# Two edits to VectorE's program order at the joints between head pairs

## The chip, the core and the metric

The kernel runs on one core of a Trainium2 chip. The metric is the device time in microseconds (us) of one execution. Each engine (TensorE for matmuls, VectorE, ScalarE, GpSimd, and SyncE, which issues the DMAs) runs its own list of instructions strictly in the order in which the program writes them; the engines meet only through semaphores, so an instruction that waits holds back everything behind it on its engine.

## The reference

One decoder block over 1024 tokens of 1024 channels, in float32. The input is normalised and projected once; the columns of that projection feed three kinds of attention heads of 64 channels and a gate.

```python
h = rms_norm(x, g_in); proj = h @ w_in
qA, kA, vA, qB, kB, vB, qM, gate, qI, kI, wI = split(proj)
oA = dilated_mixture_attention(qA, kA, vA, slopes_a)   # 8 heads, causal, three (window, dilation) patterns
oB = dsa_attention(qB, kB, vB, qI, kI, wI, slopes_b)   # 4 heads, causal, top 256 keys of an indexer; shared k, v
oM = memory_attention(qM, kM, vM)                      # 4 heads over 256 memory tokens
o = concat(oA, oB, oM) * silu(gate)
out = rms_norm(x + o @ w_out, g_final)
```

Each attention is a softmax over scores plus a distance penalty, times the values.

## The kernel before

**Steps.** After an opening part (norms, transposes, indexer scores; until about 130 us) the 16 heads are worked off in eight pairs, p = 0 to 7, in the order M0, A0, A1, A2, A3, B0, B1, M1. Each pair has eight steps, i = 0 to 7, one for each tile of 128 queries: step s = 8p + i. A causal pair has i + 1 tiles of 128 keys in position i, a memory pair always two. A step with over four key tiles is called wide; its probabilities are transposed in two chunks. All engines loop over the steps, and each has its own hand-written order in a step.

**TensorE** in step s (L1663 to L1697): the scores of s (`scores`, L1528; it waits until VectorE has taken in both halves' scores of s - 1), then the transposes of the probabilities of s - 1 (`turn_prob`, chunk 0), then projection work that belongs to a later pair (`fill`, L1403, 24 matmuls; where s - 1 has two chunks, 12 matmuls, `turn_prob` of chunk 1, 12 matmuls), then the values of s - 1 (`values`, L1567; needs the transposed probabilities copied to SBUF), and after each fourth step the transposes of the inverse sums (`turn_sums`).

**Which projection falls in which step** (`SLOT`, `projection_of_step`): the next pair's keys in positions 0 and 1, this pair's gate in 2 and 3, the next pair's values in 4 and 5, the next pair's queries in 6 and 7. Each is done in two halves of 512 tokens, b = 0 and 1, one for each step. In pair 4 the next queries lie in positions 5 and 7; pair 5 has no projection in positions 0 and 1; in pair 6 other halves lie there; pair 7 has none, its steps carry the output projection.

**The bank of a half** (`bank_ids`, L513): it accumulates in the second half of `s_ps[0]` if the step is even and has up to four key tiles, and in `j_ps` otherwise. Before `fill` writes a bank, it waits that the last half in that bank has been taken out: `wait_evacuated` waits for ScalarE's copy (semaphore `j_free`) and for VectorE's `split_low` of all halves up to that one (semaphore `j_split`). Query and key halves are kept as a high part, which ScalarE rounds, and a low part, which VectorE's `split_low` (L1108) forms as bank minus high part; for a B pair's queries it is two instructions of 64 partitions, otherwise one of 128.

**ScalarE** in step s: copies the transposed probabilities of the pair's first head (`copy_probT`, L970), takes the exponents of s for both heads (`exponent`), and takes out the projection half (`evacuate`).

**VectorE** in step s (L1327 to L1364): the masked biases of s for both heads (`add_bias`; it reads the scores and writes the negated maximum), the copy of the second head's transposed probabilities of s - 1 (`copy_probT`, L1273), in a wide step between the two biases; then the inverse sums (`invert_sums`), the first portion of the top-k choice (`choose_portions`), chunk 1's copy, `finish_group` (L1292: two products of 128 x 512, the first on TensorE's transposed sums; it releases `linv_used`, on which `turn_prob` of the next step waits), `split_low` of the step's half, and the second portion of the choice. The choice is a chain of small instructions, each waiting for the one before it; it runs from step 1 into pair 4.

**GpSimd** forms the low part of each weight tile (L711) and masks (L762, L765).

Of the kernel before, what the change touches and what calls it, by code (L numbers as in the profile page):

```python
# [19 lines left out]
NT = T // P  # L20
# [24 lines left out]
STEPS = NP * NT  # L45
# [6 lines left out]
def w_tiles():  # L52


    def q_tile(p):
        g, j, _ = PAIRS[p]
        return "q", p, [({"A": C_QA, "B": C_QB, "M": C_QM}[g] + P * j, P)]

    out = [("kIwI", None, [(C_KI, DH), (C_WI, H_I)])]
    out += [("qI", j, [(C_QI + P * j, P)]) for j in range(H_I // 2)]  # L60
    out += [q_tile(0)]
    for p, (g, j, f) in enumerate(PAIRS):
        follows = PAIRS[p + 1][:2] if p + 1 < NP else None
        if follows and follows[0] == "A":
            out += [("k", p + 1, [(C_KA + P * follows[1], P)])]
        if follows == ("B", 0):
            out += [("kvB", p + 1, [(C_KB, DH), (C_VB, DH)])]

        out += [("gate", q, [(C_GATE + P * PAIRS[q][2], P)]) for q in GATES_WITH.get(p, [p])]
        if follows and follows[0] == "A":  # L70
            out += [("v", p + 1, [(C_VA + P * follows[1], P)])]
        if follows:
            out += [q_tile(p + 1)]
    return out


W_TILES = w_tiles()
# [14 lines left out]
def query_scale(p, a):  # L92

    return -(DH ** -0.5) / (slope_of(p, a) if PAIRS[p][0] == "B" else 1.0)
# [13 lines left out]
def pair_of_step(s):  # L108
    return s // NT, s % NT


def key_tiles(s):
    p, i = pair_of_step(s)
    return MT if PAIRS[p][0] == "M" else i + 1


def chunks(s):

    n = key_tiles(s)
    return [range(c, min(c + 4, n)) for c in range(0, n, 4)]  # L120
# [18 lines left out]
def projection_of_step(s):  # L139

    p, i = pair_of_step(s)
    if p == NP - 2:
        kind, b = ENDING.get(i, (None, None))
        return (W_OF[kind], b) if kind else None
    if p == LAST_A and i in LAST_A_QUERIES:
        return W_OF["q", p + 1], LAST_A_QUERIES.index(i)
    for what, at in SLOT.items():
        if (what, p) == ("q", LAST_A):
            continue
        w = W_OF.get((what, p if what == "gate" else p + 1))  # L150
        if w is not None and w >= PRE_W and i in (at, at + 1) and (what, p) != ("gate", NP - 1):
            return w, i - at

    if (p, i) in LAST_GATE_AT:
        return W_OF["gate", NP - 1], LAST_GATE_AT.index((p, i))
    return None
# [150 lines left out]
def build_program(nc, x, mem, g_in, g_mem, w_in, w_mem, w_out, g_final, dist_tab, a_tab, out):  # L307
    with ExitStack() as ctx:
# [194 lines left out]
        use_number = {u: m for m, u in enumerate(uses)}  # L503
# [3 lines left out]
        for m, (kind, _, _) in enumerate(uses):  # L507
            if m < n_pre:
                bank_ids.append(2 if kind == "wturn" else sum(b < 2 for b in bank_ids) % 2)
            else:  # L510

                s = steps_of_uses[m - n_pre]
                bank_ids.append(3 if key_tiles(s) <= 4 and s % 2 == 0 else 0)  # L513

        def bank_of(m):
            return [j_ps[:, :], o_ps[:, :], turn_banks[4], s_ps[0][:, HALF:T]][bank_ids[m]]

        def first_token(m):


            kind, w, b = uses[m]
            return FIRST_TOPK * P if kind == "w" and W_TILES[w][0] == "qI" and b == 0 else 0
# [4 lines left out]
        def is_split(m):  # L527
            kind, w, _ = uses[m]
            if kind == "w":
                return W_TILES[w][0] in ("kIwI", "qI", "k", "kvB", "q")  # L530
            return kind == "mem" and w < 2
# [511 lines left out]
        def _(dve):  # L1043
# [64 lines left out]
            def split_low(m):  # L1108

                kind, w, b = uses[m]  # L1110
                bank = bank_of(m)
                if kind == "mem":
                    dve.wait_ge(j_free, m + 1)
                    dve.scalar_tensor_tensor(out=km[:, w, 1, :], in0=bank[:, 0:N_MEM], scalar=1.0,
                                             in1=km[:, w, 0, :].bitcast(F32), op0=ALU.mult,
                                             op1=ALU.subtract).then_inc(j_split, 1)
                    return
                what, p, _ = W_TILES[w]
                at = first_token(m)
                cut = slice(HALF * b + at, HALF * b + HALF)  # L1120
                dve.wait_ge(j_free, m + 1)

                def part(dst, rows, hi, scale=1.0):
                    return dve.scalar_tensor_tensor(out=dst, in0=bank[rows, at:], scalar=scale, in1=hi.bitcast(F32),  # L1124
                                                    op0=ALU.mult, op1=ALU.subtract)

                lower, upper, both = slice(0, DH), slice(DH, P), slice(0, P)
                if what in ("kIwI", "kvB"):
                    part(kk_b[lower, 1, cut], lower, kk_b[lower, 0, cut])
                    last = part(kk_b[upper, 1, cut], lower, kk_b[lower, 0, cut])  # L1130
                elif what == "k":
                    slot = K_SLOT[p % 2]
                    last = part(qk[both, slot + 1, cut], both, qk[both, slot, cut])
                elif what == "qI":
                    part(q_i[upper, 2 * p, cut], lower, q_i[lower, 2 * p, cut], DH ** -0.5)
                    last = part(q_i[lower, 2 * p + 1, cut], upper, q_i[upper, 2 * p + 1, cut], DH ** -0.5)
                elif PAIRS[p][0] != "B":
                    hi, lo = qk[:, Q_SLOT[p], cut], qk[:, Q_SLOT[p] + 1, cut]
                    last = part(lo, both, hi, query_scale(p, 0))
                else:  # L1140
                    hi, lo = qk[:, Q_SLOT[p], cut], qk[:, Q_SLOT[p] + 1, cut]
                    part(lo[lower, :], lower, hi[lower, :], query_scale(p, 0))
                    last = part(lo[upper, :], upper, hi[upper, :], query_scale(p, 1))
                last.then_inc(j_split, 1)
# [15 lines left out]
            for what, u, k in idx_schedule(uses):  # L1160
# [4 lines left out]
                i, h = IDX_UNITS[u]  # L1165
# [76 lines left out]
            def choose_portions(s, place):  # L1242
                for n, slot in CHOICE_AT.get((s, place), []):
                    choose(IDX_TILES[n], slot)
# [28 lines left out]
            def copy_probT(s, c):  # L1273
                g = CHUNK0[s] + c
                dve.wait_ge(pt_done[1], g + 1)
                if g >= 2:
                    dve.wait_ge(pv_done, g - 1)
                n = len(chunks(s)[c])
                dve.tensor_copy(probT[:, g % 2, 1, 0:n, :], pt_ps[1][:, 0:n, :]).then_inc(pt_ready[1], 1)  # L1279
# [43 lines left out]
            def final_norm(t):  # L1323
                dve.scalar_tensor_tensor(out=y_rows[t], in0=y_rows[t], scalar=stat[:, 3, t:t + 1], in1=gf_row,
                                         op0=ALU.mult, op1=ALU.mult).then_inc(y_final, 1)

            for s in range(STEPS + 1):  # L1327
                p, i = pair_of_step(s)
                early = FILL_OUT.get(s, (None, None, None))
                wide = s < STEPS and key_tiles(s) > 4  # L1330
                if s < STEPS:
                    add_bias(s, 0)
                if s < STEPS and not wide:
                    add_bias(s, 1)
                if s >= 1:
                    copy_probT(s - 1, 0)
                if wide:
                    add_bias(s, 1)
                if s >= 1 and (s - 1) % 4 == 3:
                    invert_sums(pair_of_step(s - 1)[0], (s - 1) % NT // 4)  # L1340
                choose_portions(s, 0)
                if early[0]:
                    add_out(*early[0])
                if s >= 1 and len(chunks(s - 1)) == 2:
                    copy_probT(s - 1, 1)
                if early[1]:
                    add_out(*early[1])
                if s == STEPS:
                    start_norm(0, 0, len(EARLY_ROWS))
                if s >= 1 and (s - 1) % 4 == 3:  # L1350
                    finish_group(pair_of_step(s - 1)[0], (s - 1) % NT // 4)
                if s == STEPS:
                    dve.wait_ge(gf_in, 16)
                    for t in EARLY_ROWS:
                        final_norm(t)
                if early[2]:
                    add_out(*early[2])
                if s < STEPS and projection_of_step(s) and is_split(use_number["w", *projection_of_step(s)]):
                    split_low(use_number["w", *projection_of_step(s)])
                choose_portions(s, 1)  # L1360
                if s in REACH_AT:
                    largest(IDX_TILES[REACH_AT[s]])
                if s in SETTLED_AT:
                    settle(IDX_TILES[SETTLED_AT[s]])  # L1364
# [378 lines left out]
```

## Time and profile before

| | us |
|---|---|
| median of 3 runs | 725.63 (723.6 to 726.18) |
| the profiled execution, its own time | 725.79 |
| its span, first to last instruction | 724.0 |
| TensorE busy in the span | 679.1 (94%) |
| VectorE busy | 422.6 (58%) |
| ScalarE busy | 333.0 (46%) |
| GpSimd busy | 146.6 (20%) |

The mean granted clock of TensorE is 0.988 of full speed. A row of the timeline gives start, duration, engine, line, output and inputs, count, and in brackets how long the engine had been idle before it and what released it.

### The profile page before, as it was taken

How to read it: one execution, taken by the hardware profiler on the slowest of the kernel's cores; microseconds unless marked ns; L12 is line 12 of the kernel's file. 1: busy time of each engine (PE TensorE's matmuls, PEld its weight loads, DVE VectorE, ACT ScalarE, POOL GpSimd, SP SyncE). 2: the span in 40 equal slices, each digit the busy share in tenths (PEclk: the TensorE clock that was granted, in tenths of full speed). 3: DMA queues.
4: the chain of work that ended last, by engine and by line, in shares of the span. 5: the costliest groups of instructions: out<-in, count | busy, mean ns of one | idle time of the engine just before them, and what ended most of it. 6: DMA issues, size and time to landing. Idle time of an engine off the chain costs nothing.

```text
span 724.0 us, 11587 instructions
## 1 busy us (share of the span) xinstructions
PE 679.1 (94%) x4287; PEld 542.6 (75%) x4287; DVE 422.6 (58%) x985; ACT 333.0 (46%) x629; POOL 146.6 (20%) x96
## 2 busy tenths in 40 slices
PE   5999999999999999999988999999999999999992
PEld 4778887777777777777766787777888777777771
DVE  3947874397788477976698564552343354122245
ACT  5777653343335443534253434653563585112224
POOL 2021110111323022221124113310111156212102
PEclk9999999999999999999999999999999999999997
DMA  8511121111311131112111121101110416510004
GB/s 297 146 47 52 30 64 24 30 29 45 88 45 44 31 88 44 30 45 88 44 31 44 32 78 49 49 2 44 44 30 20 171 52 223 166 34 23 1 34 198
DMA packets 51863, 47.71 MB, mean 66 GB/s; under 512 B 5712, under 2 KB 44640, under 8 KB 51808
## 3 DMA queue, kind: packets, MB, share of 16 engines
q1 hardware_dynamic: 51808, 46.97, 21.3%
q8 instruction: 35, 0.57, 0.3%
q14 instruction: 20, 0.16, 0.1%
HBM read 39.62 MB, written 7.34 MB: 65 GB/s over the span
## 4 chain that ended last, share of the span: by engine, by line
PE 47%; DVE 12%; issue 3%; ACT 1%; DVEq 0%; ACTq 0%
PE j_ps L1438 13%; PE o_ps L1590 6%; PE pt_ps L1564 6%; PE s_ps L1640 5%; PE s_ps L1438 5%; PE s_ps L1493 4%; PE j_ps L1640 4%; DVE unread L1193 3%; PE s_ps L1646 1%; DVE probT L1279 1%; DVE tk L1194 1%; PE j_ps L1646 1%; DVE prob L1270 1%; PE pt_ps L1612 1%; DVE tk L1196 1%
## 5 line engine op out<-in xcount | busy, mean ns | idle before, releaser
L1438 PE MATMUL j_ps<-h_hi,w_hl 128*128 128x512 f32 (+2 forms) x656 | 213.6, 391 | 3.1 <-DVE h_lo L1068 1.2
L1438 PEld LDWEIGHTS j_ps<-h_hi,w_hl 128*128 128x128 f32 (+1 forms) x656 | 121.5, 186 | 28.7 <-issue 3.1
L711 POOL TENSOR_TENSOR w_hl<-w_raw,w_hl 128x1024 fp32r<-128x1024 f32 (+1 forms) x29 | 69.1, 2384 | 330.0 <-ACT w_hl L814 311.2
L988 ACT ACTIVATE prob<-prob,nmax 128x256 f32<-128x256 f32 (+7 forms) x128 | 90.0, 704 | 85.6 <-DVE nmax L1270 70.3
L1438 PE MATMUL j_ps<-h_lo,w_hl 128*128 128x512 f32 (+2 forms) x328 | 125.5, 383 | 0.0
L976 ACT ACTIVATE probT<-pt_ps 128x512 f32<-128x512 f32 (+3 forms) x88 | 41.3, 469 | 121.5 <-PE pt_ps L1564 120.9
L1564 PE MATMUL pt_ps<-ident,prob 128*128 128x128 f32 x496 | 74.7, 283 | 10.3 <-DVE gate L1297 4.9
L1564 PEld LDWEIGHTS pt_ps<-ident,prob 128*128 128x128 f32 x496 | 55.5, 142 | 28.0 <-issue 20.9
L1438 PE MATMUL s_ps<-h_hi,w_hl 128*128 128x512 f32 x224 | 74.5, 401 | 0.9 <-ACT qk L850 0.9
L1438 PEld LDWEIGHTS j_ps<-h_lo,w_hl 128*128 128x128 f32 (+1 forms) x328 | 61.2, 187 | 11.1
L1193 DVE TENSOR_SCALAR_CACHE_REDUCE unread<-idx,tk 128x384 uint8<-128x384 f32 (+5 forms) x72 | 67.8, 942 | 1.3
L1270 DVE CUSTOM_DVE_ANT_0 prob<-s_ps,bias 128x128 f32<-128x128 f32 (+7 forms) x64 | 47.0, 753 | 24.7 <-PE s_ps L1493 20.9
L1279 DVE COPY probT<-pt_ps 128x512 f32<-128x512 f32 (+3 forms) x88 | 46.7, 530 | 15.5 <-PE pt_ps L1564 15.0
L1124 DVE SCALAR_TENSOR_TENSOR qk<-j_ps,qk 128x512 fp32r<-128x512 f32 (+2 forms) x29 | 18.4, 635 | 54.3 <-ACT qk L850 39.3
L1438 PEld LDWEIGHTS s_ps<-h_hi,w_hl 128*128 128x128 f32 x224 | 42.7, 191 | 9.6 <-ACT qk L850 1.1
L1173 DVE SCALAR_TENSOR_TENSOR idx<-prob,w_i,idx 128x384 f32<-128x384 f32 (+5 forms) x42 | 41.9, 1039 | 10.2 <-ACT prob L926 10.1
L1438 PE MATMUL s_ps<-h_lo,w_hl 128*128 128x512 f32 x112 | 44.1, 394 | 0.0
L1590 PE MATMUL o_ps<-probT,v_sb 128*64 128x128 f32 x576 | 38.6, 278 | 3.5 <-DVE probT L1279 3.5
L1590 PEld LDWEIGHTS o_ps<-probT,v_sb 128*64 128x64 f32 x576 | 30.9, 136 | 14.3 <-issue 14.1
L1270 DVE CUSTOM_DVE_ANT_0 prob<-s_ps,idx 128x384 f32<-128x384 f32 (+5 forms) x24 | 21.0, 886 | 31.9 <-PE s_ps L1493 31.9
L1493 PE MATMUL s_ps<-qk 64*128 64x512 f32 (+3 forms) x288 | 35.2, 366 | 0.0
L1640 PE MATMUL s_ps<-h_hi,w_hl 128*128 128x512 f32 x96 | 31.9, 400 | 0.0
(242 smaller groups left out, 1071.6 us busy)
## 6 DMA issues: line engine op xcount, KB each, us to landing
w_raw<-in_w_in_dram SPq DMA_DIRECT2D x27, 512.0 KB, 4.1
idx<-in_x_dram SPq DMA_DIRECT2D x8, 512.0 KB, 6.2
bias<-in_a_tab_dram SPq DMA_DIRECT2D x8, 512.0 KB, 4.5
mixed_scratch<-gate SPq DMA_DIRECT2D x12, 256.0 KB, 2.6
bias<-in_x_dram SPq DMA_DIRECT2D x4, 512.0 KB, 6.5
probT<-in_w_mem_kv_dram SPq DMA_DIRECT2D x4, 512.0 KB, 6.3
bias<-in_w_out_dram SPq DMA_DIRECT2D x4, 512.0 KB, 3.8
out_dram<-idx SPq DMA_DIRECT2D x4, 512.0 KB, 4.2
```

The source lines that it names most:

```text
L711: pool.tensor_tensor(w_hl[:, w % 2, 1, :, 0:n], raw_of(w)[:, :, 0:n], w_hl[:, w % 2, 0, :, 0:n].bitcast(F32), ALU.subtract).then_inc(w_lo_ ...
L976: act.activation(probT[:, g % 2, 0, 0:n, :], pt_ps[0][:, 0:n, :], ACT.Copy).then_inc(pt_ready[0], 1)
L988: act.activation(prob[:, a, s % 2, 0:n], prob[:, a, s % 2, 0:n], ACT.Exp, scale=-1.0, bias=nmax[:, a, s % 2:s % 2 + 1], accum_out=lsum[:, ...
L1173: dve.scalar_tensor_tensor(out=x_slice(i), in0=relu[u % 4][:, 0:n], scalar=wt, in1=x_slice(i), op0=ALU.mult, op1=ALU.add).then_inc(idx_add ...
L1193: link(dve.tensor_scalar(unread[:, 0:n], xs, level, None, ALU.is_ge, ALU.add, accum_out=count))
L1270: dve.tensor_tensor_reduce(dst, s_ps[a][:, 0:n], table, scale, 3e38, ALU.add, ALU.min, low_out).then_inc(biased[a], 1)
L1279: dve.tensor_copy(probT[:, g % 2, 1, 0:n, :], pt_ps[1][:, 0:n, :]).then_inc(pt_ready[1], 1)
L1438: last = pe.matmul(bank[0:n, at:], a[:, k, 0:n], c[:, k, HALF * b + at:HALF * b + HALF], start=(k == 0 and q == 0), stop=(k == KD - 1 and ...
L1493: last[a] = pe.matmul(banks[a][:, keys], q[rows, tile], k[rows, keys], start=(m == 0), stop=(m == 2))
L1564: last = pe.transpose(pt_ps[a][:, n, :], prob[:, a, s % 2, P * k:P * k + P], ident[:, :])
L1590: last = pe.matmul(o_ps[DH * a:DH * a + DH, at], v, probT[:, g % 2, a, n, :], start=(k == 0), stop=(k == nk - 1))
L1640: pe.matmul(bank, a[:, p, :], wo_half(c, p, b), start=(p == 0 and q == 0), stop=False)
```

## The change

In steps whose position is 0 or 1 (all such steps but s = 0, so 15 of them; none is wide) VectorE's copy of the second head's transposed probabilities of s - 1, chunk 0, stands ahead of both biases of s. And where position 7 holds the second half (b = 1) of the next pair's queries, VectorE's `split_low` of it is issued in the step after, in position 0 of the next pair, behind `finish_group`, and ahead of that step's own `split_low` if there is one. This is so at the end of pairs 0 to 5. No other engine's program changes, and no instruction is added or removed.

```diff
+            def splits_late(s):
+                p, i = pair_of_step(s)
+                piece = projection_of_step(s)
+                return i == NT - 1 and piece is not None and W_TILES[piece[0]][0] == "q" and piece[1] == 1
+
             for s in range(STEPS + 1):
                 ...
+                copy_first = s >= 1 and s < STEPS and not wide and pair_of_step(s)[1] < 2
+                if copy_first:
+                    copy_probT(s - 1, 0)
                 if s < STEPS:
                     add_bias(s, 0)
                 if s < STEPS and not wide:
                     add_bias(s, 1)
-                if s >= 1:
+                if s >= 1 and not copy_first:
                     copy_probT(s - 1, 0)
                 ...
-                if s < STEPS and projection_of_step(s) and is_split(use_number["w", *projection_of_step(s)]):
+                if s >= 1 and splits_late(s - 1):
+                    split_low(use_number["w", *projection_of_step(s - 1)])
+                if s < STEPS and projection_of_step(s) and not splits_late(s) and \
+                        is_split(use_number["w", *projection_of_step(s)]):
                     split_low(use_number["w", *projection_of_step(s)])
```

## Rows read from the trace of the kernel before

**Rows 1.** The page, part 1: engine, busy us (share of the span), instructions.

```profile
PE 679.1 (94%) x4287; PEld 542.6 (75%) x4287; DVE 422.6 (58%) x985; ACT 333.0 (46%) x629; POOL 146.6 (20%) x96
```

**Rows 2.** The waits: who waited for whom, us in total, times, longest.

```profile
DVE qk L1124 <- ACT qk L850: 42.5, 11, 6.5
PE o_ps L1590 <- DVE probT L1279: 7.5, 9, 1.8
```

**Rows 3.** The timeline around step 9, TensorE and VectorE.

```profile
200.32 0.47 PE L1438 MATMUL j_ps<-h_hi,w_hl 128*128 128x512 f32 x1
...
200.53 0.68 DVE L1124 SCALAR_TENSOR_TENSOR qk<-s_ps,qk 128x512 fp32r<-128x512 f32 x1
...
206.76 0.69 DVE L1124 SCALAR_TENSOR_TENSOR qk<-j_ps,qk 128x512 fp32r<-128x512 f32 x1 [1.51 <-ACT qk L846]
```

**Rows 4.** The timeline between steps 16 and 17, VectorE and TensorE.

```profile
274.15 0.69 DVE L1297 TENSOR_TENSOR gate<-pt_ps,gate 128x512 f32<-128x512 f32 x1 [4.54 <-PE pt_ps L1612]
...
274.99 0.42 PE L1564 MATMUL pt_ps<-ident,prob 128*128 128x128 f32 x2 [0.40 <-DVE gate L1297]
275.24 0.47 PE L1438 MATMUL j_ps<-h_hi,w_hl 128*128 128x512 f32 x1
...
275.49 0.68 DVE L1124 SCALAR_TENSOR_TENSOR qk<-s_ps,qk 128x512 fp32r<-128x512 f32 x1
```

**Rows 5.** The timeline between steps 32 and 33.

```profile
431.57 0.47 PE L1438 MATMUL j_ps<-h_hi,w_hl 128*128 128x512 f32 x1
...
431.82 1.37 DVE L1124 SCALAR_TENSOR_TENSOR kk_b<-s_ps,kk_b 64x512 fp32r<-64x512 f32 x2
```

**Rows 6.** The timeline: TensorE's stalls in steps 19, 21 and 27.

```profile
296.56 0.88 PE L1590 MATMUL o_ps<-probT,v_sb 128*64 128x128 f32 x12 [0.69 <-DVE probT L1279]
...
309.50 0.30 PE L1564 MATMUL pt_ps<-ident,prob 128*128 128x128 f32 x1 [1.52 <-DVE gate L1297]
...
374.18 0.55 PE L1590 MATMUL o_ps<-probT,v_sb 128*64 128x128 f32 x6 [1.76 <-DVE probT L1279]
```

**Rows 7.** Stretches: length, busy us of PE, PEld, DVE, ACT, POOL, granted clock.

```profile
274.20:296.50 22.30, 21.27 (x114) 16.29 (x112) 20.37 (x53) 6.72 (x17) 6.66 (x4) 1.00 0.23 60
350.40:374.10 23.70, 21.32 (x114) 16.30 (x112) 22.79 (x54) 6.70 (x17) 3.57 (x2) 1.00 0.21 57
```

**Rows 8.** The timeline between steps 48 and 49.

```profile
558.15 0.69 DVE L1301 TENSOR_TENSOR gate<-o_ps,gate 128x512 f32<-128x512 f32 x1
...
558.51 0.47 PE L1438 MATMUL j_ps<-h_hi,w_hl 128*128 128x512 f32 x1
```

**Rows 9.** The timeline of steps 40 and 41, without a projection.

```profile
482.39 1.39 DVE L1124 SCALAR_TENSOR_TENSOR qk<-j_ps,qk 64x512 fp32r<-64x512 f32 x2 [1.85 <-ACT qk L854]
...
484.24 0.69 DVE L1279 COPY probT<-pt_ps 128x512 f32<-128x512 f32 x1
...
485.07 0.63 PE L1564 MATMUL pt_ps<-ident,prob 128*128 128x128 f32 x4 [1.02 <-ACT prob L988]
...
489.09 0.69 DVE L1301 TENSOR_TENSOR gate<-o_ps,gate 128x512 f32<-128x512 f32 x1
...
490.38 0.28 DVE L1279 COPY probT<-pt_ps 128x128 f32<-128x128 f32 x1
...
490.77 0.44 PE L1590 MATMUL o_ps<-probT,v_b 128*64 128x128 f32 x4 [1.06 <-DVE probT L1279]
491.14 0.61 PE L1493 MATMUL s_ps<-kk_b,qk 64*128 64x384 f32 x4
```

**Rows 10.** The timeline of step 56, VectorE and TensorE.

```profile
602.54 1.19 DVE L1289 COPY linv<-lsum 128x512 f32<-128x512 f32 x1
603.65 0.68 DVE L1279 COPY probT<-pt_ps 128x512 f32<-128x512 f32 x1
...
604.47 0.33 PE L1590 MATMUL o_ps<-probT,v_b 128*64 128x128 f32 x2 [0.26 <-DVE probT L1279]
```

**Rows 11.** The timeline at 306 us, GpSimd and VectorE.

```profile
306.24 2.37 POOL L711 TENSOR_TENSOR w_hl<-w_raw,w_hl 128x1024 fp32r<-128x1024 f32 x1 [11.07 <-ACT w_hl L814]
...
306.26 2.37 DVE L1221 SCALAR_TENSOR_TENSOR cut<-cut 128x8 f32<-128x8 f32 x1
```

**Rows 12.** Two stretches with TensorE's clock below full, columns as in Rows 7.

```profile
375.70:379.10 3.40, 3.40 (x20) 3.03 (x17) 3.22 (x7) 3.06 (x4) 0.40 (x1) 0.50 0.02 5
...
491.70:495.10 3.40, 3.40 (x14) 2.71 (x11) 1.47 (x5) 1.57 (x5) 0.00 (x0) 0.51 0.55 148
```

## The prediction, made before the changed kernel ran

> **What bounds the kernel now.** The page's first part comes first: TensorE is busy 679.1 of 724.0 us, VectorE 422.6 [rows 1]. TensorE's program sets the time, and an edit to VectorE counts only where TensorE waits for it. So I read the waits next. VectorE waits for ScalarE's copies ahead of its query splits for 42.5 us in all [rows 2]; nobody pays for that. TensorE waits for VectorE's probability copies nine times, 7.5 us in the group with the longest [rows 2]. Then I read the timeline at each joint between two pairs, TensorE beside VectorE, to see which of these waits lie in positions 0 and 1, where the change acts. Most don't: they stand in steps 19, 21 and 27 [rows 6], which the change does not touch.
>
> **The late split.** The moved instruction releases a bank. Step 7 of a pair is odd, so the second query half accumulates in `j_ps`; position 0 is even with few keys, so its half goes to the other bank; position 1 is odd again and takes `j_ps`. The fill of position 1 therefore waits for `j_split` of the query half. Before, that split was done a step earlier. Now it stands behind `finish_group`, which itself waits for the transposed sums, the last thing that TensorE does in position 0. Between there and the fill TensorE has only a score group and a short transpose.
>
> The price is read at each joint. Between steps 16 and 17 the fill starts at 275.24. VectorE issues its next split at 275.49, right behind `finish_group` [rows 4]. That slot now goes to the query split: 275.49 + 0.68 = 276.17. From the end of a VectorE instruction to the start of the matmul that it releases the same rows give 274.99 - (274.15 + 0.69) = 0.15. The fill starts at 276.32 instead of 275.24: 1.08 late. The same at step 9: 200.53 + 0.68 + 0.15 - 200.32 = 1.04 [rows 3]; at step 33: 431.82 + 0.69 + 0.15 - 431.57 = 1.09 [rows 5], taking one instruction of 0.69 since pair 4 is an A pair; step 25 has the same gap of a quarter of a microsecond between fill and slot, so 1.08. At step 49 the queries are a B pair's, two instructions of 1.39 together [rows 9]: the slot begins 0.60 behind the start of the second product, 558.75, and 558.75 + 1.39 + 0.15 - 558.51 = 1.78 [rows 8]. In all five: 6.07.
>
> Not all of it reaches the end, since TensorE stalls later for VectorE anyway. VectorE is resynchronised at each joint (4.54 idle ahead of `finish_group` [rows 4]) and its own delay behind it is one split, 0.69, not 1.08. In steps 17 to 19 and 25 to 27 it then has no slack: 20.37 busy in 22.30 us, and 22.79 in 23.70, the rest being the gaps between chained small instructions [rows 7]. There the next stall (0.69 and 1.76 [rows 6]) shrinks by 1.08 - 0.69 = 0.39. Behind step 9 there is a pause of 1.51 for ScalarE [rows 3], so nothing comes back; I take the same for step 33. So 1.04 + 0.69 + 0.69 + 1.09 + 1.78 = 5.29. VectorE's freed 0.69 in position 7 is worth nothing: it lands in the 4.54 idle. Bounds: 4 if every joint gives back as much as steps 17 and 25 and more, 6.1 if none does.
>
> **The copy first, and steps 40 and 41.** In 12 of the 15 steps a fill of 24 matmuls or other projection work lies between the transposes and the values, and neither the copy's nor the biases' place matters: the next reader of the biases comes behind that fill. If that cover were gone, each such step would lose two biases, 0.3 to 0.8. Steps 40, 41 and 56 have no fill. In step 40 TensorE waits 1.02 ahead of its last transposes; the row names ScalarE, but VectorE's copy ends only at 484.24 + 0.69 = 484.93 and the transposes start 0.14 later, because two splits stand ahead of it from 482.39 to 483.78 [rows 9]. With the splits gone and the copy in front it starts with the transposes' end, about 483.16, and the transposes at 483.99: 1.08 earlier. The chunk 1 copy, behind biases and sums, becomes the next late one and takes back 0.42; gain 0.66. In step 41 the two splits (1.39) stand behind `finish_group` and ahead of the copy; the copy leaves the two biases (0.68) behind it. The copy comes 0.69 - 0.66 = 0.03 off where it was, so the values start as before; the biases end 0.86 later than before, and the next scores, which need them and started at 491.14, start about 0.3 late. Steps 40 and 41 together: 0.3 lost; bounds -1.1 (only the gain) and +1.4 (only the splits).
>
> Step 56: the biases end before the transposes do today, so copying first pushes both biases (0.76) behind the copy. The inverse-sum copy that follows took 1.19 against 0.43 as elsewhere, held up on its own account [rows 10]; if that hold has a fixed end, all is absorbed. Between 0 and 0.75 at the stall of 0.26 [rows 10] I take 0.2.
>
> **Sum.** 5.29 + 0.3 + 0.2 = 5.8 on the profiled execution's 725.79: 731.6. That execution is 0.16 above the median of the runs shown, so I forecast 731.5.
>
> **Rivals.**
> First, the clock. It fell to half in two stretches of 3.4 us, each behind a thin stretch of TensorE: one behind the stall of 1.76, one behind steps 40 and 41 [rows 6, 9, 12]. A fall costs half of 3.4, 1.7, where TensorE is the bound. The new stall of 1.04 to 1.78 lies 0.4 behind an existing one, so steps 9 and 49 could each draw a fall: 731.5 + 3.4 = 734.9. Against it: the stall of 1.52 in step 21 drew none [rows 6].
>
> Second, fewer collisions between VectorE and GpSimd. At 306.26 a tiny VectorE instruction lasts 2.37 and ends with GpSimd's, which had started 0.02 ahead [rows 11]; the stall of 1.52 follows from it. A shift of 0.69 in VectorE could step out of such collisions: the stalls 0.69, 1.52 and 1.76 [rows 6] would go, 731.5 - 4.0 = 727.5. It decides if GpSimd's work moves with TensorE and not with VectorE. Against it: GpSimd is released by ScalarE, which waits for VectorE's biases, so both move together.
> The Trainium skill (SBUF — State Buffer, "Who interferes with whom") says that a VectorE instruction with two SBUF inputs is fully blocked by a GpSimd instruction that reads SBUF and started first. The trace agrees by the 2.37 above. By that rule alone a shift of 0.03 us in issue order would decide over 1.5 us.
>
> Third, and on the other side: VectorE's backlog is the bound and the edits relieve it. Its place is the run of stalls in steps 11 to 29: with 0.69 less ahead of each joint the choice would run ahead and TensorE's 7.5 us of waits for copies [rows 2] would go: 731.5 - 7.5 = 724.0, not slower. It decides if VectorE has no pause ahead of `finish_group`. It has 4.54 [rows 4].
>
> Fourth, the change doesn't do what it says: the fills of position 1 are in a bank that the late split doesn't hold. Then only steps 40, 41 and 56 are left: 725.63 + 0.5 = 726.1. The bank rule read in the code speaks against it.
>
> **Chances.** Forecast 0.62, with falls of the clock 0.20, fewer collisions 0.10, backlog 0.04, no hold 0.04. 0.5%, or 3.6 us, is about what this kernel's measurement can tell from no change. Slower by more than that (above 729.3): the forecast 0.62, the clock 0.20 and 0.06 of the collisions, 0.88. Within: the other 0.04 of the collisions, the unheld case 0.04 and half of the backlog 0.02, 0.10. Faster: the other half, 0.02. The range, 727.8 to 735.2, holds the forecast with the bounds of its terms, part of the collisions and two falls of the clock; it leaves out the backlog, the unheld case and the whole gain of the collisions.
>
> **What would show it.** The timeline of the changed kernel shows in steps 9, 17, 25, 33 and 49 a first matmul into `j_ps` idle for 1.0 to 1.8 and released by VectorE's L1124 line (with a shifted number); steps 19 and 27 have smaller stalls than before; in step 40 the stall of 1.02 is gone or nearly; step 41 keeps its 1.06 or grows, and the stall ahead of the scores behind it is new. It would be wrong if the first matmuls of these steps start without a stall, or if the time between two joints changes by more than the stalls at them.

## The result and the profile after

The changed kernel is slower: 733.73 us median of 6 runs (732.8 to 734.55) against 725.9 of 6 runs of the kernel before. The ratio is 1.0099 with a 95% interval of 1.0079 to 1.0120, so 7.2 us (5.7 to 8.7) are lost. (The ratios in this document are estimated from all the runs of both kernels and are not quotients of two medians; the medians here lie 7.8 apart.) The forecast was 731.5 within 727.8 to 735.2, a loss of 5.8.

The profiled execution took 734.27 us, 8.48 more than that of before. The busy times hardly moved, so the loss is waiting and slower clock (the page: engine, busy us, share, instructions; compare [rows 1]):

```profile
PE 680.9 (93%) x4287; PEld 542.8 (74%) x4287; DVE 421.6 (58%) x985; ACT 333.3 (46%) x629; POOL 146.5 (20%) x96
```

The waits have one row that the trace before does not have, and the wait for copies is hardly changed, 8.7 against 7.5 [rows 2] (changed kernel; TensorE's and VectorE's lines below L1340 now stand 13 further down, so L1438 is L1451):

```profile
PE o_ps L1603 <- DVE probT L1279: 8.7, 8, 1.9
...
PE j_ps L1451 <- DVE qk L1124: 4.9, 5, 1.6
```

Five times, up to 1.6 us: the five joints. The timeline of the changed kernel shows them at steps 9, 17, 33 and 49; step 25 reads like step 17 (start, duration, engine, line; in brackets the idle time and its releaser). VectorE at step 9 comes first, where two L1124 stand where one stood in [rows 3]:

```profile
200.03 0.69 DVE L1301 TENSOR_TENSOR gate<-o_ps,gate 128x512 f32<-128x512 f32 x1
200.64 0.68 DVE L1124 SCALAR_TENSOR_TENSOR qk<-j_ps,qk 128x512 fp32r<-128x512 f32 x1
201.23 0.68 DVE L1124 SCALAR_TENSOR_TENSOR qk<-s_ps,qk 128x512 fp32r<-128x512 f32 x1
```

```profile
200.14 0.45 PE L1577 MATMUL pt_ps<-ident,prob 128*128 128x128 f32 x2 [0.42 <-DVE gate L1297]
201.42 0.47 PE L1451 MATMUL j_ps<-h_hi,w_hl 128*128 128x512 f32 x1 [0.82 <-DVE qk L1124]
...
277.58 0.47 PE L1451 MATMUL j_ps<-h_hi,w_hl 128*128 128x512 f32 x1 [0.85 <-DVE qk L1124]
...
298.45 0.33 PE L1603 MATMUL o_ps<-probT,v_sb 128*64 128x128 f32 x2 [0.24 <-DVE probT L1279]
...
376.68 0.33 PE L1603 MATMUL o_ps<-probT,v_sb 128*64 128x128 f32 x2 [1.70 <-DVE probT L1279]
...
435.11 0.47 PE L1451 MATMUL j_ps<-h_hi,w_hl 128*128 128x512 f32 x1 [0.85 <-DVE qk L1124]
...
565.35 0.47 PE L1451 MATMUL j_ps<-h_hi,w_hl 128*128 128x512 f32 x1 [1.55 <-DVE qk L1124]
```

The stall at 298.45 is the one that was 0.69 at 296.56 [rows 6]: here part of the hold comes back. The one at 376.68, in step 27, is nearly as long as its 1.76 of before. The next fence is TensorE in steps 40 to 42 of the changed kernel, for [rows 9]. The 1.02 ahead of the second transposes is gone (they are inside the x8), the wait ahead of the values has grown from 1.06 to 1.87, and the wait ahead of the scores is new:

```profile
486.99 1.21 PE L1577 MATMUL pt_ps<-ident,prob 128*128 128x128 f32 x8 [0.30 <-issue]
488.13 2.13 PE L1603 MATMUL o_ps<-probT,v_sb 128*64 128x128 f32 x32
...
494.08 0.48 PE L1603 MATMUL o_ps<-probT,v_b 128*64 128x128 f32 x4 [1.87 <-DVE probT L1279]
494.94 1.01 PE L1506 MATMUL s_ps<-kk_b,qk 64*128 64x384 f32 x4 [0.38 <-DVE nmax L1270]
```

And the clock (stretches of the changed kernel: length, busy us of PE, PEld, DVE, ACT, POOL, granted clock). Behind step 41 the low level of 1.2 GHz lasts twice as long as in [rows 12], and there is a new fall behind step 49; the one at 375.7 is gone:

```profile
494.40:501.10 6.70, 6.32 (x23) 4.87 (x21) 1.86 (x9) 2.67 (x9) 0.00 (x0) 0.50 0.28 73
566.10:569.40 3.30, 3.30 (x9) 2.56 (x8) 0.28 (x2) 1.06 (x4) 0.00 (x0) 0.50 0.92 344
375.70:379.10 3.40, 2.42 (x28) 2.08 (x29) 3.19 (x10) 3.37 (x7) 0.40 (x1) 1.00 0.02 5
```

How much later each stretch of steps begins than in the trace before, read from the first score matmul of the step in both traces:

| from step to step | lateness before, after it | gained or lost | what it is |
|---|---|---|---|
| start to 9 | 0, 0.11 | 0.11 | |
| 9 to 10 | 0.11, 1.11 | 1.00 | hold |
| 10 to 17 | 1.11, 1.31 | 0.20 | stall of step 11, 1.00 against 0.78 (differs from run to run) |
| 17 to 25 | 1.31, 1.92 | 0.61 | hold 1.03, given back 0.45 at step 19 |
| 25 to 33 | 1.92, 2.51 | 0.59 | hold 1.01, given back 0.38 in step 26, 0.04 in step 27 |
| 33 to 40 | 2.51, 3.57 | 1.06 | hold |
| 40 to 41 | 3.57, 2.59 | -0.98 | stall of 1.02 gone |
| 41 to 42 | 2.59, 3.80 | 1.21 | splits ahead of the copy, and 0.38 ahead of the scores |
| 42 to 43 | 3.80, 5.12 | 1.32 | the longer fall of the clock |
| 49 to 50 | 5.12, 8.49 | 3.37 | hold 1.72, the rest the new fall |
| 50 to the end | 8.49, 8.50 | 0.01 | |

### The profile page after: what moved, and what is told of

Read it like the earlier page. It is cut to its first block, busy times and chain, and to the rows that moved or that the text cites. A ratio compares the mean times of both kernels' runs of the same rounds, so it can differ in the third digit from the quotient of the medians.

```text
span 732.5 us, 11582 instructions
## 1 busy us (share of the span) xinstructions
PE 680.9 (93%) x4287; PEld 542.8 (74%) x4287; DVE 421.6 (58%) x985; ACT 333.3 (46%) x629; POOL 146.5 (20%) x96
## 4 chain that ended last, share of the span: by engine, by line
PE 46%; DVE 13%; issue 3%; ACT 1%; DVEq 0%; ACTq 0%
PE j_ps L1451 13%; PE o_ps L1603 6%; PE pt_ps L1577 6%; PE s_ps L1451 5%; PE s_ps L1653 5%; PE s_ps L1506 4%; PE j_ps L1653 4%; DVE unread L1193 3%; PE s_ps L1659 1%; DVE qk L1124 1%; DVE probT L1279 1%; DVE tk L1194 1%; DVE prob L1270 1%; PE j_ps L1659 1%; PE pt_ps L1625 1%
## 5 line engine op out<-in xcount | busy, mean ns | idle before, releaser
L1451 PE MATMUL j_ps<-h_hi,w_hl 128*128 128x512 f32 (+2 forms) x656 | 214.6, 393 | 8.0 <-DVE qk L1124 4.9
L1451 PEld LDWEIGHTS j_ps<-h_hi,w_hl 128*128 128x128 f32 (+1 forms) x656 | 121.9, 187 | 34.7 <-issue 8.8
L1451 PE MATMUL j_ps<-h_lo,w_hl 128*128 128x512 f32 (+2 forms) x328 | 126.0, 384 | 0.0
L1451 PE MATMUL s_ps<-h_hi,w_hl 128*128 128x512 f32 x224 | 75.2, 405 | 0.9 <-ACT qk L850 0.9
L1451 PEld LDWEIGHTS j_ps<-h_lo,w_hl 128*128 128x128 f32 (+1 forms) x328 | 61.5, 188 | 11.3
L1451 PEld LDWEIGHTS s_ps<-h_hi,w_hl 128*128 128x128 f32 x224 | 43.1, 192 | 9.7 <-ACT qk L850 1.1
L1124 DVE SCALAR_TENSOR_TENSOR qk<-j_ps,qk 128x512 fp32r<-128x512 f32 (+2 forms) x29 | 18.3, 632 | 48.2 <-ACT qk L850 38.0
L1451 PE MATMUL s_ps<-h_lo,w_hl 128*128 128x512 f32 x112 | 44.4, 396 | 0.0
```

The lines of the kernel that those rows point to most:

```text
L1451: last = pe.matmul(bank[0:n, at:], a[:, k, 0:n], c[:, k, HALF * b + at:HALF * b + HALF], start=(k == 0 and q == 0), stop=(k == KD - 1 and ...
```

## The experiments

The kernel before ran again beside them: a median of 726.18 us (29 runs) beside the first four, 727.13 (27 runs) beside the next three. Each ratio is against the runs beside it.

**Only the split late.** `copy_first = False`, the rest as in the changed kernel.

> Only the query split moves; the copies keep their place behind the biases. If the held fill is the cause, steps 9, 17, 25, 33 and 49 each show a first matmul into j_ps idle for 0.8 to 1.6 us as in the changed kernel, step 40's stall of 1.02 is gone, and step 41 waits longer than in the changed kernel, since the splits and the biases both stand ahead of its copy: 733.5 to 734.5 us. If the reordered copy is the cause (rival), this kernel is back at the time before, 726 us.

Measured 734.34 us (730.87 to 736.7), ratio 1.0107 (1.0071 to 1.0142). The trace has the same five stalls, 0.82 at step 9 and 1.55 at step 49, and at step 41 the wait of 2.48 that splits and biases in front of the copy give. TensorE's waits in steps 9, 41 and 49 of this kernel:

```profile
200.69 0.47 PE L1451 MATMUL j_ps<-h_hi,w_hl 128*128 128x512 f32 x1 [0.82 <-DVE qk L1124]
...
494.16 0.44 PE L1603 MATMUL o_ps<-probT,v_b 128*64 128x128 f32 x4 [2.48 <-DVE probT L1279]
...
563.72 0.61 PE L1451 MATMUL j_ps<-h_hi,w_hl 128*128 128x512 f32 x1 [1.55 <-DVE qk L1124]
```

The late split alone brings a loss as large as that of both edits.

**Only the copies first.** `splits_late` returns False.

> Only the copies go first; the query split stays in its step. If the held fill is the cause: no j_ps stall, step 40's stall of 1.02 shrinks by 0.4 and step 41's of 1.06 by 0.7, so about 1 us faster than before, 724.8 us, and 723.1 if TensorE's clock does not fall behind step 41. Rival (the reordered copy delays the biases and so the following steps): about 733 us.

Measured 724.87 us (722.94 to 727.88), ratio 0.9980 (0.9963 to 0.9998): a gain of 1.5 us, at the edge of what can be told from nothing. TensorE in steps 40 to 42 of this kernel: the waits of 1.02 and 1.06 [rows 9] are 0.60 and 0.43, and the biases, now behind the copy, come 0.29 late for the scores:

```profile
484.86 0.63 PE L1577 MATMUL pt_ps<-ident,prob 128*128 128x128 f32 x4 [0.60 <-DVE probT L1279]
...
490.13 0.44 PE L1603 MATMUL o_ps<-probT,v_b 128*64 128x128 f32 x4 [0.43 <-DVE probT L1279]
490.87 0.45 PE L1506 MATMUL s_ps<-kk_b,qk 64*128 64x384 f32 x2 [0.29 <-DVE nmax L1270]
```

Nothing else in the trace answers to the twelve other moved copies. Its stall in step 11 is 1.29 against 0.78, but the last of the kernels below, which has the program of the kernel before up to step 39, shows 1.55 there.

**Both edits, the split ahead of finish_group.**

```diff
+                if s >= 1 and splits_late(s - 1):
+                    split_low(use_number["w", *projection_of_step(s - 1)])
                 if s >= 1 and (s - 1) % 4 == 3:
                     finish_group(pair_of_step(s - 1)[0], (s - 1) % NT // 4)
                 ...
-                if s >= 1 and splits_late(s - 1):
-                    split_low(use_number["w", *projection_of_step(s - 1)])
```

> Both edits, but the moved split stands ahead of finish_group in position 0, not behind it: one statement's place. If the hold is the distance from finish_group to the fill, all five j_ps stalls are gone, because VectorE idles 0.7 to 4.5 us at this place; step 40 gains 1.0, step 41 up to 0.7: 724.3 us, and 722.5 without a fall of the clock. Rival (it is enough that the split comes a step later): as the changed kernel, 733.7 us.

Measured 724.51 us (721.92 to 728.14), ratio 0.9980 (0.9957 to 1.0002). The split is as late as in the changed kernel by the step, and not one j_ps stall is left. VectorE and TensorE between steps 16 and 17 of this kernel, for [rows 4]; the split lies in the pause, which is 3.95 instead of 4.54, and the fill follows its transposes without a wait:

```profile
269.15 0.68 DVE L1124 SCALAR_TENSOR_TENSOR qk<-j_ps,qk 128x512 fp32r<-128x512 f32 x1
273.78 0.69 DVE L1297 TENSOR_TENSOR gate<-pt_ps,gate 128x512 f32<-128x512 f32 x1 [3.95 <-PE pt_ps L1625]
```

```profile
274.62 0.42 PE L1577 MATMUL pt_ps<-ident,prob 128*128 128x128 f32 x2 [0.40 <-DVE gate L1297]
274.87 0.47 PE L1451 MATMUL j_ps<-h_hi,w_hl 128*128 128x512 f32 x1
```

Its profiled execution took 726.39, and in step 29 it fell 3.8 us behind, by something that its expectation did not name. VectorE and GpSimd of this kernel at 386 us, and TensorE behind them:

```profile
386.07 2.09 DVE L1194 SCALAR_TENSOR_TENSOR tk<-tk,rungs 128x1 f32<-128x1 f32 x1
388.19 2.27 DVE L1196 SCALAR_TENSOR_TENSOR tk<-tk,rungs 128x1 f32<-128x1 f32 x1
```

```profile
386.06 2.08 POOL L765 TENSOR_TENSOR idx<-idx,dist 128x896 f32<-128x896 f32 x1
388.11 2.34 POOL L711 TENSOR_TENSOR w_hl<-w_raw,w_hl 128x1024 fp32r<-128x1024 f32 x1
```

```profile
391.33 1.00 PE L1577 MATMUL pt_ps<-ident,prob 128*128 128x128 f32 x6 [4.53 <-DVE gate L1297]
```

Two instructions of one column, which take 0.16 and 0.22 elsewhere, start 0.01 and 0.08 behind a GpSimd instruction and end with it. TensorE stalls for 4.53 there, against 0.56 and 1.56 in the same step before. The kernel's twelve runs spread over 6 us, so this kernel cannot be told from the one before, though it is clearly better than the changed one.

**VectorE's load without the wait.** The kernel before, with

```diff
+                if s in EXTRA:          # {8: 1, 16: 1, 24: 1, 32: 1, 48: 2}, behind finish_group
+                    for _ in range(EXTRA[s]):
+                        link(dve.tensor_scalar(unread[:, 0:HALF], dist[:, 0:HALF], 0.0, None, ALU.is_ge))
```

> The kernel before with one extra VectorE instruction of 128 x 512 (about 0.7 us, into a scratch tile that only VectorE writes; two of them in step 48) behind finish_group of steps 8, 16, 24, 32 and 48, on which nobody waits. If only the wait hurts, it costs just where VectorE has no slack, 0.7 at step 19 and 0.7 at step 27: 727.3 us. Rival (VectorE's load behind the joint is the price, with or without the wait): six times 0.7, 730.2 us.

Measured 727.31 us (724.46 to 731.77), ratio 1.0018 (0.9993 to 1.0044). The added instruction took 0.42, not 0.7. TensorE's stalls of this kernel at steps 17, 18 and 19 (its lines stand 5 further down):

```profile
275.95 0.47 PE L1443 MATMUL j_ps<-h_hi,w_hl 128*128 128x512 f32 x1
...
289.19 0.33 PE L1595 MATMUL o_ps<-probT,v_sb 128*64 128x128 f32 x2 [0.39 <-DVE probT L1279]
...
297.73 0.33 PE L1595 MATMUL o_ps<-probT,v_sb 128*64 128x128 f32 x2 [0.70 <-DVE probT L1279]
```

No fill is held. The lateness grows by 0.45 in step 18 and by 0.45 in step 26, one added instruction each time, where VectorE has no slack, and by nothing at steps 9, 33 and 49. It also grows by 0.43 in step 29, but that follows a collision of 2.15 where the kernel before has 1.69, and these vary from run to run. So in the trace VectorE's load costs its own length in the stretches of [rows 7], and at steps 9, 33 and 49 only the wait costs. The times alone don't say so: the median fell on the expectation by luck, since the instruction was shorter than assumed; six times its true length would give 728.7, inside the interval, and so is no change at all.

**The split between the two products of finish_group.**

```diff
                 dve.tensor_tensor(gates(p)[:, cut], pt_ps[0][:, :, :]..., gates(p)[:, cut], ALU.mult).then_inc(linv_used, 1)
+                if g == 1 and p < NP - 1 and splits_late(p * NT + 7):
+                    split_low(use_number["w", *projection_of_step(p * NT + 7)])
                 dve.wait_ge(linv_used, groups[0])
                 ...
-                if s >= 1 and splits_late(s - 1):
-                    split_low(use_number["w", *projection_of_step(s - 1)])
```

> The changed kernel with the late split one instruction earlier: between finish_group's two products, so 0.73 us nearer to the end of the sums. If the hold is the distance between the sums and the split, each j_ps stall shrinks by 0.73: from 0.82 and 0.85 to about 0.1 in steps 9, 17, 25 and 33, from 1.55 to about 0.8 in step 49; steps 40 and 41 stay as in the changed kernel: 730.7 us. Rival (it is enough that the split is late, wherever): 733.7 us.

Measured 729.81 us (727.79 to 731.45), ratio 1.0038 (1.0024 to 1.0052), against 1.0099 of the changed kernel, and 0.9 below what was expected. One instruction of 0.73 out of the way takes 0.72 off each stall. Its first fills of steps 17 and 49 (the first with a wait of 0.13, too short for a bracket):

```profile
276.88 0.47 PE L1451 MATMUL j_ps<-h_hi,w_hl 128*128 128x512 f32 x1
...
563.27 0.47 PE L1451 MATMUL j_ps<-h_hi,w_hl 128*128 128x512 f32 x1 [0.83 <-DVE qk L1124]
```

**One joint alone.** The kernel before with the split of step 47 late and nothing else: `splits_late` returns `s == 47`, `copy_first = False`.

> The kernel before with the query split late at the end of pair 5 alone, and no copy moved. If the joints add up, only step 49 is held, by 1.7 us, and TensorE's clock may fall behind it for 3.4 us, another 1.7 in those executions: 727.7 to 729.5 us. Rival (the joints' losses are absorbed by later waits): 726 us.

Measured 728.36 us (727.49 to 731.48), ratio 1.0027 (1.0015 to 1.0040), 2.0 us. Step 49 shows the 1.55 of the changed kernel, the lateness grows there by 1.72, and nothing comes back up to the end. The clock did not fall behind it in the profiled execution. First fill, and the stretch from it on:

```profile
560.86 0.47 PE L1451 MATMUL j_ps<-h_hi,w_hl 128*128 128x512 f32 x1 [1.55 <-DVE qk L1124]
```

```profile
560.90:564.90 4.00, 4.00 (x18) 3.33 (x19) 0.87 (x5) 1.10 (x4) 0.00 (x0) 1.00 0.91 319
```

**The edits only where nothing covers them.** `splits_late` returns `s == 39`, with the split ahead of `finish_group`, and `copy_first = s in (40, 41)`.

> The kernel before with the edits only where no projection work covers them: copies first in steps 40 and 41 alone, and the split of step 39 in step 40 ahead of finish_group. Step 40 gains 1.0, step 41 0.3 to 0.7, and TensorE's clock keeps full speed behind step 41 in more executions: 724.5 us. Rival (moving VectorE by a few hundredths changes its collisions with GpSimd more than the edits bring): no difference from before, 726 us.

Measured 723.72 us (722.75 to 728.6), ratio 0.9964 (0.9948 to 0.9980): 2.6 us faster than the kernel before (1.5 to 3.8), and the lowest ratio of all, though its interval overlaps those of the two others below 1. TensorE in steps 40 to 42, and the clock behind them:

```profile
486.06 1.21 PE L1577 MATMUL pt_ps<-ident,prob 128*128 128x128 f32 x8 [0.30 <-issue]
...
491.73 0.44 PE L1603 MATMUL o_ps<-probT,v_b 128*64 128x128 f32 x4 [0.45 <-DVE probT L1279]
492.46 0.62 PE L1506 MATMUL s_ps<-kk_b,qk 64*128 64x384 f32 x4 [0.29 <-DVE nmax L1270]
```

```profile
491.00:495.00 4.00, 3.26 (x22) 2.42 (x22) 2.69 (x11) 2.71 (x9) 0.48 (x1) 1.00 0.64 169
```

From step 40 to step 42 it gains 1.32 on the kernel before, and another 1.5 by step 49, where the fall of [rows 12] is missing. The runs without a profile agree: the median of their mean granted clocks is 0.992, against 0.988 for the kernel before beside them. Its profiled execution, 725.63, is 1.6 later behind step 29 than ahead of it, with a collision there like the one above (1.95 us at 387.8).

**Second traces of both kernels.**

> The changed kernel once more, unaltered, for a second trace. If the hold is fixed by the program, the five j_ps stalls are the same to 0.05 us; the falls of TensorE's clock outside the tail may differ in place and length, and the execution's time with them by 1.7 us each: 731 to 735 us. Rival (the falls are fixed by the program too): the same falls at 494 and 566 us.

> The kernel before once more, unaltered, for a second trace. If falls of the clock and collisions between VectorE and GpSimd make its spread from run to run, the stalls of 0.4 at the joints repeat to 0.05 us while a fall or a stall between 206 and 400 us differs: 723 to 730 us.

The changed kernel again: 736.08 us, with first-fill stalls of 0.82, 0.85, 0.85, 0.85 and 1.55. Falls of the clock lie behind step 41 (again 6.8 us long) and behind step 49, and a third one at 393.3 behind a stall of 2.45 in step 29. The kernel before again: 726.46 us, with the same two falls as in [rows 12], at 376.2 and 492.2. The changed kernel's 736.08 lies above the expected 731 to 735. The falls behind steps 41 and 49, which I expected to differ, came back at the same places in both traces of the changed kernel; the one in step 29 did not. Two traces don't show that every execution has them: a fall of 3.4 lowers the mean granted clock by 0.0023, and that of the six runs of the changed kernel lies between 0.986 and 0.989.

## Why the prediction was right, and where it was off

**The bound and the place.** Right: TensorE's program sets the time (93% busy after the change), and the two edits cost and gain only at the joints and in the stretches behind steps 17 and 25. Away from them VectorE counts too, by its collisions with GpSimd, whatever the edits.

**The hold of the fill.** Right in mechanism and size. Forecast 1.04, 1.08, 1.08, 1.09 and 1.78; measured, as the start of the fill against before less the lateness so far, 0.99, 1.03, 1.03, 1.03 and 1.72. Each is 0.05 or 0.06 short because the fill starts 0.10 behind the split's end (200.64 + 0.68 = 201.32 and 201.42 in the rows of step 9), where the forecast took 0.15 from another instruction. The idle times are 0.82 to 1.55 and not the 1.0 to 1.8 that were named as the sign, since the first 0.17 or so of the hold passes while TensorE's transposes still run. The experiments show the cause from three sides: the late split without the copies has it, the late split ahead of `finish_group` doesn't, and 0.73 less of distance makes each stall 0.72 shorter.

**What comes back.** Right in size, wrong in one place: 0.39 each forecast at the stalls of steps 19 and 27; 0.45 came back at step 19, but behind step 25 it was a stall of 0.31 in step 26 that went away (0.38), and the 1.76 of step 27 gave back 0.04. Nothing came back behind steps 9 and 33, as said. A further 0.2 at step 11 was lost to a collision of 1.84 instead of 1.64 us; that need not be an effect of the edits, since four traces that share one program up to step 39 have 1.64, 1.74, 1.91 and 2.41 there.

**Steps 40 and 41.** The net was right, 0.3 forecast and 0.23 found (-0.98 and +1.21), by two errors that cancelled. The failed step is "The chunk 1 copy ... takes back 0.42". It took back nothing: the copy started at 488.33, 0.34 behind the inverse-sum copy's start and not after its full 0.43 plus a pause, and TensorE did not stop for it. So the gain was 0.98 and not 0.66. (The 1.08 from which 0.66 was reckoned was also more than the whole stall of 1.02.) The second error ran the other way, in step 41. From the end of `finish_group` to the end of the biases the forecast allows 0.86 + 0.66 = 1.52 more than before. The rows, VectorE of the changed kernel and then of the kernel before, give 494.79 - 492.28 = 2.51 against 490.46 - 489.70 = 0.76, so 1.75 more: behind the splits and behind the copy the next instruction starts 0.03 and 0.04 after the recorded end, where those of before start 0.07 or 0.08 ahead of it.

```profile
492.28 1.38 DVE L1124 SCALAR_TENSOR_TENSOR qk<-j_ps,qk 64x512 fp32r<-64x512 f32 x2
493.69 0.29 DVE L1279 COPY probT<-pt_ps 128x128 f32<-128x128 f32 x1
494.02 0.42 DVE L1270 CUSTOM_DVE_ANT_0 prob<-s_ps,dist 128x256 f32<-128x256 f32 x1
...
494.37 0.42 DVE L1270 CUSTOM_DVE_ANT_0 prob<-s_ps,dist 128x256 f32<-128x256 f32 x1
```

```profile
489.70 0.41 DVE L1270 CUSTOM_DVE_ANT_0 prob<-s_ps,dist 128x256 f32<-128x256 f32 x1
...
490.04 0.42 DVE L1270 CUSTOM_DVE_ANT_0 prob<-s_ps,dist 128x256 f32<-128x256 f32 x1
```

**Step 56.** Forecast 0.2, found nothing; the lateness is 8.5 on both sides of it. The condition that the prediction named for this held: the inverse-sum copy's hold has a fixed end. It ends at 603.73 before [rows 10] and 8.52 later here, with 0.51 in place of 1.19:

```profile
611.74 0.51 DVE L1289 COPY linv<-lsum 128x512 f32<-128x512 f32 x1
```

**The clock.** This is the term that was left out of the sum and put into a rival of 0.20. The table puts 1.32 on the longer fall behind step 41 and 1.65 (3.37 - 1.72) on the fall behind step 49; without them it adds up to 8.50 - 2.97 = 5.5, against the forecast's sum of 5.8, and 0.3 of that 5.5 (up to step 9, and step 11) belongs to no term of the forecast: its own terms measured 5.2. The rival named steps 9 and 49; at step 9 no trace shows a fall, behind step 41 it named none. The second sign of being wrong that the prediction gave is met here: from step 42 to the joint at step 49 the time changed by 1.32 with no stall to show for it. The fall at 375.7 that went away gave nothing back: in the changed kernel TensorE stalled for 1.31 in step 28 instead, waiting for VectorE, and the lateness stayed at 2.5.

```profile
386.55 0.33 PE L1603 MATMUL o_ps<-probT,v_sb 128*64 128x128 f32 x2 [1.31 <-DVE probT L1279]
```

All eleven traces divide this way: five have a fall near 376 and no stall in step 28, the other six have no fall there and a stall of 1.31 to 1.33. From step 27 to step 29 all of them take the same time to 0.1. So this fall cost nothing, and not half its length: TensorE would have waited for VectorE there. The median's loss, 7.2, lies between the sum without falls and the profile's 8.5.

**The other rivals.** The backlog rival and the one that the fill is not held are refuted by the traces. Fewer collisions did not come: in all eleven traces the ones at about 290, 306 and 367 us recur with the same lengths. Only those at 215 and in step 29 vary, from run to run as well.

## What to carry to other kernels

Before moving an instruction later on an engine that has slack, list which semaphore it raises and who waits for the count, also for the reuse of a buffer: here the reader of the split was far off, but the next writer of its bank started 0.25 us ahead of the split's new place (275.24 and 275.49, [rows 4]). Slack is a place and not a total: ahead of VectorE's own wait for TensorE an instruction was free (4.54 us of idle here); behind that wait it cost 1.0 to 1.7 us where TensorE waited for that very instruction, its own length where VectorE had no slack up to TensorE's next wait (0.45 at steps 18 and 26), and nothing elsewhere (the instructions added at steps 8, 32 and 48). An order that helps where nothing covers it should be made only there; three of fifteen steps were such, and the edits in two of them, with the split ahead of the wait, brought 2.6 us (1.5 to 3.8), of which 1.5 is in the trace a fall of the clock that did not come.

## What the runs showed of the hardware that I had not expected

A thin stretch of TensorE can be answered by a fall of twice the length: behind step 41 it was 3.4 us in both traces of the kernel before and in that with the joint of step 49 alone (idle 1.06 or 1.07 ahead of the values), and 6.8 in both of the changed one (1.87 and 1.80) and in that with the split between the products (1.67). It was absent in the three kernels with 0.43 to 0.45 idle there. But 2.48 of idle with only the split late drew 3.4 and not 6.8, the same 1.07 of idle drew no fall in the kernel with VectorE's added load, and the stall of 1.55 in step 49 drew one in three traces and none in the trace with that joint alone. In step 29 stalls of 2.29, 2.45 and 4.53 drew a fall, 2.32 and 2.36 none. What decides between these was not settled; the stall's length alone does not.

Single collisions of VectorE with GpSimd were larger than the edits under study: in step 29 two in a row took 4.36 us (2.09 + 2.27) for two instructions that take 0.38 elsewhere, and whether they meet there differs between runs of one kernel. The Trainium skill (SBUF — State Buffer, "Who interferes with whom") says that a VectorE instruction with two inputs in SBUF contends with a GpSimd instruction that reads SBUF, that the ports which they share are an exclusive lock, and that the order of issue decides which of them is blocked. The trace of step 29 agrees: both VectorE instructions have two such inputs, started 0.01 and 0.08 us behind GpSimd's and ended 0.02 and 0.01 behind its end.
